# One decoder layer on one core: the stores of the gate matrix are issued by SP behind the loads of the weight units, in place of ScalarE

## The reference, cut to what matters

```
sc = einsum('thpk,hpnk->thpn', q, sub_keys)         # 8 heads, 2 sides, 128 keys
va, ia = top_k(sc[:, :, 0], 16);  vb, ib = top_k(sc[:, :, 1], 16)
top, flat = top_k((va[..., :, None] + vb[..., None, :]).reshape(n_tok, 8, 256), 16)
expert = take(ia, flat // 16) * 128 + take(ib, flat % 16)
gate = softmax(top)
act = gelu(einsum('tkd,td->tk', w_down[expert], x))
out = einsum('tk,tkd->td', gate * act, w_up[expert])
```

## Time and profile before

| | |
|---|---|
| median of 3 runs | 1560.04 us (1559.79 to 1560.24) |
| the profiled execution's own time | 1560.45 us |
| its span, first to last instruction | 1558.7 us |
| mean granted TensorE clock | 0.995 |
| PE busy | 1540.3 us (99%) |
| DVE, ACT, POOL busy | 1133.6, 638.9, 735.2 us |
| q1, q0, q10 moved | 253.86, 134.23, 21.32 MB |

### The profile page before, as it was taken

How to read it: one execution, slowest core, us unless ns; L and a number is a source line. 1 busy time by engine, 2 the same in 40 slices (tenths; PEclk the granted TensorE clock), 3 DMA queues, 4 the chain that set the end, 5 groups by cost and what they waited for, 6 DMA issues and landing times.

```text
span 1558.7 us, 23481 instructions
## 1 busy us (share of the span) xinstructions
PE 1540.3 (99%) x8604; PEld 1389.4 (89%) x8604; DVE 1133.6 (73%) x2354; ACT 638.9 (41%) x851; POOL 735.2 (47%) x452
## 2 busy tenths in 40 slices
PE   8999999999999999999999999999999999999996
PEld 8888899888899999999999999988888888888885
DVE  5564262477999877697769763788888888888888
ACT  5323244423234456446643663343333333333333
POOL 1543572224346966777678768732222222222220
PEclk9999999999999999999999999999999999999998
DMA  8432250332245977899699879999999999999993
GB/s 313 182 107 82 95 176 28 108 136 95 81 145 190 348 273 247 317 416 334 237 350 416 305 255 337 370 372 347 334 343 334 339 342 327 353 324 344 343 382 115
DMA packets 141004, 410.84 MB, mean 264 GB/s; under 512 B 15329, under 2 KB 49377, under 8 KB 140385
## 3 DMA queue, kind: packets, MB, share of 16 engines
q1 hardware_dynamic: 97840, 253.86, 46.1%
q0 software_dynamic: 36864, 134.23, 23.7%
q10 hardware_dynamic: 6192, 21.32, 3.5%
HBM read 363.22 MB, written 46.14 MB: 263 GB/s over the span
## 4 chain that ended last, share of the span: by engine, by line
PE 88%; DVE 10%; issue 1%; DMA 0%; POOL 0%; SPq 0%; DVEq 0%; ACT 0%; ACTq 0%
PE ps L1659 11%; PE ps L1661 11%; PE ps L1660 11%; PE ps L1305 10%; PE ps L1307 10%; PE ps L1306 10%; PE ps L433 6%; PE ps L434 6%; PE ps L435 6%; PE ps L1630 1%; PE ps L1632 1%; DVE gmat L1007 1%; DVE gmat L1000 1%; DVE gmat L1001 1%; DVE gmat L1004 1%
## 5 line engine op out<-in xcount | busy, mean ns | idle before, releaser
L1516 ACT ACTIVATE w_hi<-raw 128x1024 fp32r<-128x1024 f32 x252 | 266.6, 1058 | 344.4 <-PE ps L1661 313.9
L1305 PE MATMUL ps<-b_hi,w_hi 128*128 128x384 f32 x1024 | 346.5, 338 | 0.2 <-POOL w_lo L1482 0.2
L1307 PE MATMUL ps<-b_hi,w_lo 128*128 128x384 f32 x1024 | 342.4, 334 | 0.0
L1306 PE MATMUL ps<-b_lo,w_hi 128*128 128x384 f32 x1024 | 342.2, 334 | 0.0
L1482 POOL TENSOR_TENSOR w_lo<-raw,w_hi 128x1024 fp32r<-128x1024 f32 x119 | 287.0, 2412 | 104.5 <-ACT w_hi L1516 102.8
L1490 POOL DMA_INDIRECT rows<-in_w_up,expert x128 | 144.1, 1126 | 375.9 <-DVE ps L1728 366.7
L1661 PE MATMUL ps<-w_hi,b_lo 128*128 128x512 f32 x768 | 298.8, 389 | 0.0
L1660 PE MATMUL ps<-w_lo,b_hi 128*128 128x512 f32 x768 | 298.8, 389 | 0.0
L1659 PE MATMUL ps<-w_hi,b_hi 128*128 128x512 f32 x768 | 298.8, 389 | 0.0
L1735 DVE TENSOR_TENSOR w_lo<-raw,w_hi 128x1024 fp32r<-128x1024 f32 x133 | 162.9, 1225 | 79.9 <-ACT w_hi L1516 79.9
L1694 DVE SCALAR_TENSOR_TENSOR rows<-rows,ps 128x1024 f32<-128x1024 f32 x128 | 155.5, 1219 | 88.4 <-DMA rows<-in_w_down,expert 80.8
(11 more groups left out here) (265 smaller groups left out, 2488.2 us busy)
## 6 DMA issues: line engine op xcount, KB each, us to landing
raw<-in_down_t SPq DMA_DIRECT2D x128, 512.0 KB
raw<-in_up_t SPq DMA_DIRECT2D x128, 512.0 KB
raw<-in_units SPq DMA_DIRECT2D x75, 512.0 KB, 3.3
act_d<-act_t SPq DMA_DIRECT2D x128, 192.0 KB
c<-act_d SPq DMA_DIRECT2D x128, 192.0 KB
gate_d<-gmat ACTq DMA_DIRECT2D x32, 512.0 KB
v<-gate_d SPq DMA_DIRECT2D x16, 512.0 KB
i<-gate_d SPq DMA_DIRECT2D x16, 512.0 KB
```

Source lines behind the costliest of these rows:

```text
L1305: nc.tensor.matmul(out, ring.w_hi[:, s, w], b_hi[:, c, 0:DT], start=c == 0, stop=False)
L1306: nc.tensor.matmul(out, ring.w_hi[:, s, w], b_lo[:, c, 0:DT], start=False, stop=False)
L1307: last = nc.tensor.matmul(out, ring.w_lo[:, s, w], b_hi[:, c, 0:DT], start=False, stop=c == KC - 1)
L1516: nc.scalar.activation(w_hi[:, u % W4, :], raw[:, u % W4, :], ACT.Copy).then_inc(hi_done, 1)
```

## The change

`store_piece` moves from ACT's program into SP's, with the same wait ahead of its first piece. SP issues the pieces in the same tiles, in its own order: store of `act_d[u]`, `load(u + 8)`, then the tile's pieces. The wait for `gate_stored` ahead of `gate_out` stays on ACT; SP's own wait for it at tile 104 stays too.

```diff
@@ SP
+            def store_piece(b, i):
+
+                if i == 0:
+                    sp.wait_ge(half_free, halves * (b + 1))
+                sp.dma_start(t["gate_d"][b, :, PB * i * P:(PB * i + PB) * P],
+                              gmat[:, PB * i:PB * i + PB, :].rearrange("p b j -> p (b j)")).then_inc(gate_stored, 16)
+
...
                 load(u + 2 * W4)
+                b, i = divmod(u - LEAD, BLOCK_TILES)
+                if u >= LEAD + BLOCK_TILES and b < DB and i < len(STORES):
+                    for piece in STORES[i]:
+                        store_piece(b - 1, piece)
                 if u == TILES - 24:
...
@@ ACT
-            def store_piece(b, i):
-
-                if i == 0:
-                    act.wait_ge(half_free, halves * (b + 1))
-                act.dma_start(t["gate_d"][b, :, PB * i * P:(PB * i + PB) * P],
-                              gmat[:, PB * i:PB * i + PB, :].rearrange("p b j -> p (b j)")).then_inc(gate_stored, 16)
-
...
-                if u >= LEAD + BLOCK_TILES and b < DB and i < len(STORES):
-                    for piece in STORES[i]:
-                        store_piece(b - 1, piece)
                 if u == TILES - 7:
```

## The result

The changed kernel takes 1573.59 us (median of 6 runs, 1571.28 to 1574.93) against 1560.14 us before (6 runs, 1559.77 to 1561.25). The ratio is 1.0085, 95% interval 1.0075 to 1.0095. The profiled execution of the changed kernel took 1574.08 us, its span is 1572.3 us, 13.6 more than before. So the way was right and the size was half of what came.

A forecast was written before the change was run, and what follows sets the result against it. PE was taken as the bound, so only its waits count: two stalls from late last gate stores, 6.5 us, other parts 0, on the 1560.04 us median gave 1566.5 us (chance 0.62); range 1559.8 to 1573.7.

The forecast's parts named there:

- PE is the bound, and only a wait of PE matters: Whole kernel: PE busy 1540.3 of 1558.7 us; each microsecond PE stands still is added in full.
- Place and mechanism: Tiles 60 and 92, before gate round 1: PE waits for ACT's copies, held by late gate stores, 2 to 5 us each.
- Loads and act_d no later than now: SP's queue q1 in the bursts: loads and act_d stores get no later than now, 0 us for PE.
- PE's two stalls are on the path in full: Tiles 60 and 92: both stalls add their full length, 6.5 us together; ACT isn't late again afterwards.
- The size of the stalls: Both bursts' last pieces land past ACT's deadlines: 6.5 us in all, the rounded middle of (a) and Estimate (b).
- Estimate (b): Last pieces on q1, by bytes: backlogs of 2.59 and 2.43 MB land 3.2 and 4.0 us past the deadlines, 7.2 us.
- (a): Last pieces on q1 take today's neighbouring load time, 11.85 and 10.24 us: 3.5 + 2.2 = 5.7 us of stall.
- the tail: Last piece on q1: time from bytes moved until ACT can start, taken as 3 us.
- SP comes 3 us earlier to the last piece: SP in the bursts: earlier loads bring it to the last pieces 3 us earlier, so rival A would hold.
- rival A: Same two waits of ACT: stores land in time, nothing changes; 1560.0, up to 1563 us; chance 0.27.
- B: Both whole bursts: q1 starves as gathers take half the engines; twice 14 us, 1588 us; chance 0.07.
- the side risk of block 2's picks: Block 2: a later gather would hold DVE's picks, then PE; 1 or 2 us if it goes wrong, not expected.

The follow-up runs named there:

- run 5: Kernel before, but ACT issues every piece one tile (4.1 us) later, still on its own queue; 1563.03 us, ratio 1.0019.
- run 2: Changed kernel, all stores by SP, two pieces a tile in a burst's first four tiles, so the last goes out two tiles earlier; 1565.23 us, ratio 1.003.
- run 3: Kernel before, no store moved; ACT makes the first copy in tiles 59 and 91 four times more; 1570.62 us, ratio 1.0066.
- run 6: Kernel before, no store moved; ACT makes the first copy in tiles 59 and 91 twice more; 1564.11 us, ratio 1.0025.
- run 1: Changed kernel, but the last two pieces (14 and 15) of each burst are issued by ACT again; 1563.3 us, ratio 1.0019.
- run 4: Changed kernel, but SP issues a tile's pieces ahead of load(u + 8) instead of behind it; 1562.54 us, ratio 1.0013.
- run 7: Changed kernel, SP behind the loads, two pieces in each of the first three tiles, so the last goes out one tile earlier; 1563.69 us, ratio 1.0028.

## Why the prediction was half of it

- **PE is the bound, and only a wait of PE matters**: right. 13.1 of 13.6 us of span are lost at two places in which PE stood, in the stands and right after them.
- **Place and mechanism**: right. Gate round 1 of blocks 1 and 2, behind ACT's wait for the last piece; ACT's units come with less waiting (13.6 us), and in the bursts q10 is empty, while q1 moves 269 GB/s in 650 to 702 us, where about 290 were expected. The stores lost their own queue: 15.6 us in SP's (the change), at most 9.5 in ACT's even when issued later (run 5). The round robin of queues in the Trainium skill ("DMA: Bandwidth & Descriptors", section "Queues, rings and completion order") agrees with this. The rule in the section "Issuing engines are not separate DMA queues" of the same page of the Trainium skill, by which there would have been no change, holds here only for the sum: the engines' rate in 650 to 702 us hardly changed, 416 and 412 GB/s, but which transfer gets it did.
- **Loads and act_d no later than now**: half right. "They get no later" held for units, but ACT waits 24.9 us for act_d, where the prediction had it fall below 14.7. It stayed hidden in the change; in run 2 it didn't.
- **The step that failed, in the sum**: "PE's two stalls are on the path in full" was taken to be all of it. Each stall also brings the clock down, which nothing in the sum had: 3.2 us (runs 3 and 6).
- **The size of the stalls**, the term that was in the sum: 6.5 forecast, 9.2 measured (4.51 + 4.71), 9.9 with the second bank. Estimate (b) gave 7.2 and the mean with (a) took 0.7 off it; (a), today's load, says nothing about a queue that carries 18.78 MB in 640 to 712 us where it carried 11.23. In (b) two parts were right. In 640 to 712 us the engines moved 29.14 MB before and 28.30 in the change, 0.84 less, the number that I had taken for the late start. And the rate of q1 was 301 GB/s for my 303: it had moved 15.80 MB by 702.1 and 18.78 by 712. What was wrong is how much stood open at 702.1: of the 18.81 MB asked (10.09 + 0.33 + 8.39) not 2.59 but 3.0 MB, as q0 had by then moved 8.34 MB, where before it had moved 7.91. At 301 GB/s the 3.0 MB take 10.0 us in place of 8.5, and the tail was 3.4 us, not 3. This is the second step that failed. The second piece landed 1.1 us later than in (b) (871.30, less the 6.27 between the traces, for 863.9); that I have not taken apart.

The change in 640 to 702.1 us, then in 640 to 712:

```profile
q1 hardware_dynamic: 5398, 15.80, 65.2%
q0 software_dynamic: 2277, 8.34, 34.1%
...
q1 hardware_dynamic: 6418, 18.78, 66.6%
q0 software_dynamic: 2592, 9.44, 33.2%
```

- **SP comes 3 us earlier to the last piece** (from rival A): it came 2.3 us earlier, 699.83 for my 702.1. That did not save the deadline: q1 reached the 18.8 MB only by 712 us. B did not come, and neither did the side risk of block 2's picks: PE has no wait for them.
- **The range** ended at 1573.7 and the median lies at 1573.59 on six runs; the interval of the ratio reaches beyond it.

So the first term was sized at 0.66 of its value (6.5 of 9.9), and the second at nothing: together 6.5 of 13.1.

What stays open: what decides whether a short stand brings the clock down. Stands of 1.7 us in block 2 did (run 1) and did not (runs 4 and 7). And I have not taken apart how much of the 2.5 us of runs 1 and 5 is the idle start of the burst.

## What to carry to other kernels

When the DMA engines are full, the queue on which a transfer stands is part of its price: here the same bytes took at most 9.5 us on a queue of their own and 15.6 us behind the loads, at the same total rate. Move a store only after finding who waits for its end, and count the bytes ahead of it, including those that idle DMA engines could have moved earlier. And where TensorE bounds the kernel, a stand of it may not be paid with its length alone: look at the granted clock after it, and add what comes at half pace.

## What the runs showed of the hardware

Each of the four stands of TensorE of 2.3 to 4.7 us (the change and run 3) came with a granted clock of 0.50 for some 3 to 7 us, which cost 1.3 to 1.9 us. In three of them the clock fell only 0.2 to 0.6 us after TensorE had started again, in the fourth (block 2 of the change) during the stand. Eleven stands of 0.6 to 1.7 us had no such fall, one of 1.67 us had (run 1). Two DMA queues moved as much as three (412 and 416 GB/s). And a piece issued 4.5 us earlier on a full queue ended 4.0 us earlier (run 4 against the change); by the count of bytes there, about half of the gain came from starting the burst while the DMA engines were not yet full.
